# x's split straight from PSUM at two joins, the second half's turn half a unit later, and other banks for the HGRN values

## The reference, cut to what matters

```python
x = x + gate[:, None, :] * y            # after each mixer of the first block
...
x = _rms_norm(x, final_g)               # the first block's output
...
u = rmsnorm(h, norm1_w[l])
proj = jnp.einsum('bsd,de->bse', u, w_in[l])
...
h = h + jnp.einsum('bse,ed->bsd', mixed, w_out[l])
u2 = rmsnorm(h, norm2_w[l])
gu = jnp.einsum('bsd,df->bsf', u2, w_gate_up[l])
```

## Time and profile before

| | us |
|---|---|
| median of 3 runs (726.63 to 727.56) | 727.55 |
| the profiled execution | 727.51 |
| its span, first to last instruction | 725.7 |
| TensorE busy, matmuls / weight loads | 705.6 / 577.7 |
| VectorE busy | 501.6 |
| ScalarE busy | 380.0 |

### The profile page before, as it was taken

The page is one execution under the profiler, slowest core; times in us unless marked ns, Lnnn a source line. Parts: engine busy times, 40 slices in busy tenths (PEclk is TensorE's granted clock), DMA queues, the critical chain, the costliest instruction groups (busy, mean ns, idle before and its releaser), DMA issues.

```text
span 725.7 us, 9362 instructions
## 1 busy us (share of the span) xinstructions
PE 705.6 (97%) x3534; PEld 577.7 (80%) x3534; DVE 501.6 (69%) x727; ACT 380.0 (52%) x559; POOL 15.9 (2%) x33
## 2 busy tenths in 40 slices
PE   6999999999999999999999899999999999999996
PEld 5887877777887788788887688878888888888884
DVE  4789888787956778665658689955775555555444
ACT  5347544565544565553565654554565445444342
POOL 6000000000000000000000000000000000000000
PEclk8799999999999999999999999999999999999999
DMA  9998865676986357733444553333456655555611
GB/s 295 369 373 312 295 202 182 197 227 210 312 296 205 113 178 249 244 117 115 147 148 143 146 174 117 117 116 117 129 187 206 192 180 180 180 196 178 197 61 58
DMA packets 74476, 138.96 MB, mean 191 GB/s; under 512 B 5748, under 2 KB 18272, under 8 KB 74432
## 3 DMA queue, kind: packets, MB, share of 16 engines
q1 hardware_dynamic: 72816, 134.82, 57.3%
q10 hardware_dynamic: 736, 1.90, 0.7%
q0 software_dynamic: 880, 1.64, 0.6%
HBM read 137.31 MB, written 1.05 MB: 191 GB/s over the span
## 4 chain that ended last, share of the span: by engine, by line
PE 89%; DVE 6%; ACT 2%; issue 2%; DMA 1%; SPq 0%; DVEq 0%; ACTq 0%
PE G L382 23%; PE G L384 23%; PE G L383 22%; PE T L403 5%; PE T L771 2%; DVE wlo L1057 2%; PE T L884 2%; DVE arena L1057 1%; PE T L761 1%; PE G L493 1%; DMA arena<-in_mod_w_dram 1%; PE G L495 1%; PE G L494 1%; PE T L444 1%; ACT whi L1796 1%
## 5 line engine op out<-in xcount | busy, mean ns | idle before, releaser
L1057 DVE TENSOR_TENSOR wlo<-raw,whi 128x1024 fp32r<-128x1024 f32 x202 | 246.1, 1223 | 127.2 <-ACT whi L1796 126.5
L382 PE MATMUL G<-whi,ahi 128*128 128x512 f32 x760 | 307.8, 405 | 4.3 <-DVE wlo L1057 4.3
L384 PE MATMUL G<-whi,alo 128*128 128x512 f32 x760 | 297.0, 391 | 0.0
L383 PE MATMUL G<-wlo,ahi 128*128 128x512 f32 x760 | 296.1, 390 | 0.0
L1796 ACT ACTIVATE whi<-raw 128x1024 fp32r<-128x1024 f32 x202 | 212.9, 1060 | 123.5 <-PE G L384 108.4
L382 PEld LDWEIGHTS G<-whi,ahi 128*128 128x128 f32 x760 | 142.9, 188 | 36.9 <-DVE wlo L1057 8.9
L384 PEld LDWEIGHTS G<-whi,alo 128*128 128x128 f32 x760 | 142.6, 188 | 31.3
L383 PEld LDWEIGHTS G<-wlo,ahi 128*128 128x128 f32 x760 | 143.1, 188 | 28.0 <-issue 1.2
L1798 ACT ACTIVATE arena<-T,st 128x128 f32<-128x128 f32 (+2 forms) x56 | 21.7, 478 | 30.4 <-DVE st L1429 30.4
L1796 ACT ACTIVATE ahi<-T 128x512 fp32r<-128x512 f32 x25 | 15.0, 599 | 41.8 <-PE T L403 41.8
L403 PE MATMUL T<-head,arena 128*128 128x128 f32 x244 | 36.8, 275 | 0.0
(11 more groups left out here) (227 smaller groups left out, 606.8 us busy)
## 6 DMA issues: line engine op xcount, KB each, us to landing
raw<-in_ret_w_in_dram SPq DMA_DIRECT2D x48, 512.0 KB, 5.4
raw<-in_w_gate_up_dram SPq DMA_DIRECT2D x40, 512.0 KB, 3.6
raw<-in_mod_w_dram SPq DMA_DIRECT2D x32, 512.0 KB, 4.8
raw<-in_fox_w_in_dram SPq DMA_DIRECT2D x32, 512.0 KB, 4.8
raw<-in_w_in_dram SPq DMA_DIRECT2D x28, 512.0 KB, 3.5
raw<-in_w_down_dram SPq DMA_DIRECT2D x22, 512.0 KB, 4.3
arena<-in_mod_w_dram SPq DMA_DIRECT2D x16, 512.0 KB, 8.8
raw<-in_ret_w_out_dram SPq DMA_DIRECT2D x16, 512.0 KB, 5.6
```

What stands on the lines that cost most here:

```text
L382: e.matmul(o, ah, wh, start=first and k == 0, stop=False)
L383: e.matmul(o, ah, wl, start=False, stop=False)
L384: done = e.matmul(o, al, wh, start=False, stop=last and k == 1)
L1057: e.tensor_tensor(o, a, b, op).then_inc(sig[name], 1)
```

## The change

`x_high` on ScalarE and `x_low` on VectorE take the place of `x_act` and `x_split` for n = 4 to 11. `x_high` writes the scaled, rounded tiles straight to `ahi`; `x_low` computes tile * scale - `ahi` from PSUM, one `scalar_tensor_tensor` for each 128x128 tile, and waits for all four activations of its n. The stage isn't used any more. `ready` names one count per tile, and the T bank of these n is free only when `x_low` is through with it. In unit 1 of the second block the second turn of x's second half comes between the products of m = 0 and m = 1. `x_low(7)` stands behind the first `f_prod`, `x_high(7)` behind the first `square`, and ScalarE squares `f_prod` k one loop turn later. `hg_values` uses banks 1 and 2 by name, so the rotation behind it begins two banks earlier. The numbers computed are the same; no load is changed. (The own tiles for the forgetting attention's first chunk, `own_tiles`, are in both kernels.)

```diff
             def x_turn(src, k0, m):
...
-                t = bank(("x", n), sig["x_act"], 2 * SPLIT_ORDER.index(n) + 2)
+                p = SPLIT_ORDER.index(n)
+                t = bank(("x", n), *((sig["x_act"], 2 * p + 2) if n < 4 else (sig["x_split"], 4 * p + 4)))
...
-                for z in range(2):
-                    for k in range(2):
-                        ready[slot + k0 + 2 * z + k, m] = (sig["x_split"], 4 * p + 3 + z)
+                for k in range(4):
+                    ready[slot + k0 + k, m] = (sig["x_split"], 4 * p + (3 + k // 2 if n < 4 else 1 + k))
...
             for k in range(4):
-                unit(u, accs, 16 + 2 * k, k == 0, k == 3)
-                u += 1
-                if k == 0:
-                    for m in range(2):
-                        on_.wait_ge(sig["res1"], 2 * m + 6)
-                        x_turn(x, 4, m)
+                for m in range(2):
+                    products(u, m, accs, 16 + 2 * k, k == 0, k == 3)
+                    if (k, m) in ((0, 1), (1, 0)):
+                        on_.wait_ge(sig["res1"], 2 * k + 6)
+                        x_turn(x, 4, k)
+                u += 1
...
-                t = bank(("hg_values", m), sig["hg_norm"], 4 + m)
+                t = bank(("hg_values", m), sig["hg_norm"], 4 + m, 1 + m)
...
+            def x_low(n, slot, k0, m, scale):
...
+                on_.wait_ge(sig["x_act"], 2 * p + 2)
+                for k in range(4):
+                    b = slot + k0 + k
+                    stt(alo[:, b, ms], t[:, k * P:(k + 1) * P], scale(k0 + k), ahi[:, b, ms].bitcast(F32), ALU.mult, ALU.subtract, "x_split")
...
-            x_split(4, 16, 0, 0, stage2)
-            x_split(5, 16, 0, 1, stage2)
+            x_low(4, 16, 0, 0, lambda k: col(n1f, k))
+            x_low(5, 16, 0, 1, lambda k: col(n1f, k))
...
                 if k == 0:
-                    x_split(6, 16, 4, 0, stage2)
-                    x_split(7, 16, 4, 1, stage2)
+                    x_low(6, 16, 4, 0, lambda k: col(n1f, k))
...
                 tt(f2[:, m, cs_], x[:, m, cs_], fg[:, cs_], ALU.mult, "f_prod")
+                if k == 0:
+                    x_low(7, 16, 4, 1, lambda k: col(n1f, k))
...
+            def x_high(n, slot, k0, m, scale):
...
+                on_.wait_ge(sig["x_turned"], n + 1)
+                for k in range(4):
+                    act(ahi[:, slot + k0 + k, ms], t[:, k * P:(k + 1) * P], ACT.Copy, "x_act" if k % 2 else None, scale=scale(k0 + k))
...
-            x_act(6, stage2, 4, ACT.Copy, lambda k: col(n1f, k))
-            x_act(7, stage2, 4, ACT.Copy, lambda k: col(n1f, k))
+            x_high(6, 16, 4, 0, lambda k: col(n1f, k))
             on_.wait_ge(sig["left_turned"], 12)
             for k in range(4):
...
                 square(c, m, 1, 2 * k + 2)
-                on_.wait_ge(sig["f_prod"], k + 1)
-                on_.wait_ge(sig["sq1"], k + 1)
-                act(xn1[:, m, cs_], f2[:, m, cs_], ACT.Square, "sf1", accum=st[:, 68 + 2 * m + c:69 + 2 * m + c])
+                if k == 0:
+                    x_high(7, 16, 4, 1, lambda k: col(n1f, k))
+                if k:
+                    square_f(k - 1)
+            square_f(3)
```

More of the change, by code:

```diff
@@ L1186, in x_split @@
                     tt(alo[:, b:b + 2, ms], stage[:, (2 * p + z) % 4, :, :], ahi[:, b:b + 2, ms].bitcast(F32), ALU.subtract, "x_split")
+            def x_low(n, slot, k0, m, scale):
+                p = SPLIT_ORDER.index(n)
+                t, ms = T[bank_of["x", n]], slice(m * P, m * P + P)
+                on_.wait_ge(sig["x_act"], 2 * p + 2)
+                for k in range(4):
+                    b = slot + k0 + k
+                    stt(alo[:, b, ms], t[:, k * P:(k + 1) * P], scale(k0 + k), ahi[:, b, ms].bitcast(F32), ALU.mult, ALU.subtract, "x_split")
             stage1 = acc[:, 2048:3072].rearrange("p (z n s) -> p z n s", z=4, n=2)
@@ L1498, in _ @@
             u_out = {0: u + 1, 1: u + 3}
-            stage2 = gate[:, 0, :].rearrange("p (z n s) -> p z n s", z=4, n=2)
             ring_to(u + 2)
@@ L1719, in _ @@
             ring_to(u + 4)
-            x_split(8, 22, 0, 0, stage2)
-            x_split(9, 22, 0, 1, stage2)
+            x_low(8, 22, 0, 0, lambda k: col(n2_col, k))
+            x_low(9, 22, 0, 1, lambda k: col(n2_col, k))
             ring_to(u + 5)
@@ L1745, in _ @@
                     if c == 0 and k == 0:
-                        x_split(10, 22, 4, 0, stage2)
-                        x_split(11, 22, 4, 1, stage2)
+                        x_low(10, 22, 4, 0, lambda k: col(n2_col, k))
+                        x_low(11, 22, 4, 1, lambda k: col(n2_col, k))
                     if c == 0 and k == 2:
@@ L2114, in _ @@
             sqrt_table()
-            stage2 = gate[:, 0, :].rearrange("p (z n s) -> p z n s", z=4, n=2)
             ring_to(u + 4)
             on_.wait_ge(sig["rows_read"], 3)
-            x_act(4, stage2, 0, ACT.Copy, lambda k: col(n1f, k))
-            x_act(5, stage2, 0, ACT.Copy, lambda k: col(n1f, k))
+            x_high(4, 16, 0, 0, lambda k: col(n1f, k))
+            x_high(5, 16, 0, 1, lambda k: col(n1f, k))
             ring_to(u + 5)
@@ L2143, in turned_win, with square_f @@
                 from_four("wqk", n, (qA, kA)[n // 2][:, :, m * P:(m + 1) * P], ACT.Copy, (0.125, 1.0)[n // 2])
+            def square_f(k):
+                c, m = k // 2, k % 2
+                cs_ = slice(512 * c, 512 * c + 512)
+                on_.wait_ge(sig["f_prod"], k + 1)
+                on_.wait_ge(sig["sq1"], k + 1)
+                act(xn1[:, m, cs_], f2[:, m, cs_], ACT.Square, "sf1", accum=st[:, 68 + 2 * m + c:69 + 2 * m + c])
             ring_to(u + 2)
             u += 1
-            x_act(6, stage2, 4, ACT.Copy, lambda k: col(n1f, k))
-            x_act(7, stage2, 4, ACT.Copy, lambda k: col(n1f, k))
+            x_high(6, 16, 4, 0, lambda k: col(n1f, k))
             on_.wait_ge(sig["left_turned"], 12)
@@ L2243, in _ @@
             ring_to(u + 4)
-            x_act(8, stage2, 0, ACT.Copy, lambda k: col(n2_col, k))
-            x_act(9, stage2, 0, ACT.Copy, lambda k: col(n2_col, k))
+            x_high(8, 22, 0, 0, lambda k: col(n2_col, k))
+            x_high(9, 22, 0, 1, lambda k: col(n2_col, k))
             ring_to(u + 5)
@@ L2257, in _ @@
                     if c == 0 and k == 0:
-                        x_act(10, stage2, 4, ACT.Copy, lambda k: col(n2_col, k))
-                        x_act(11, stage2, 4, ACT.Copy, lambda k: col(n2_col, k))
+                        x_high(10, 22, 4, 0, lambda k: col(n2_col, k))
+                        x_high(11, 22, 4, 1, lambda k: col(n2_col, k))
                         on_.wait_ge(sig["left_turned"], 16)
```

## The result

The changed kernel took 721.96 us (median of 4 runs, 721.78 to 723.09) against 727.55 us (4 runs, 726.63 to 729.19): ratio 0.9916 [0.9898, 0.9935]. That is 5.6 us faster by the medians and 6.1 us by the ratio. The forecast was 721.8. Repeated on another chip it was 722.11 us (5 runs) against 727.81 (9 runs), ratio 0.9921 [0.9905, 0.9936].

What follows compares the result with a forecast made beforehand. TensorE, busy 97% of the span, was taken as the bound, so time is gained only where it waits. Join 4.9 plus HGRN banks 0.8 plus feed-forward 0 gave 5.7 us: 727.5 to 721.8 us, range 720.7 to 723.7.

Steps and rivals of the forecast that it cites:

- What bounded the kernel: Join from forgetting attention to second block: TensorE waits 5.6 of 30.3 us, mostly on a 3.64 us round trip.
- The split: VectorE's x_low from PSUM: four operations at 0.27 us pitch, 1.08 us per n; alone costs 0.16 us before first turn.
- Rival A: At x_low: short operations don't overlap, pitch 0.35 us, gain only 4.6 us, giving 722.9 us; chance 0.15.
- The turn half a unit later: Second turn of x's second half, at the join: its 0.91 us wait disappears at no cost.
- ScalarE's order: Second block's loop at the join: a ScalarE round takes some 2.2 us, under TensorE's 2.72.
- One of the prediction's signs of being wrong: At the join: rounds of over 2.8 us between whi starts would show the forecast wrong.
- The q turns: Turns of q at the join's end: put_h and q products, 5.0 us earlier, stop holding them; up to 0.35 us more.
- The banks: HGRN values in banks 1 and 2: their wait behind the last window-attention product goes, gaining 0.8 us.
- Rival C: At the HGRN values: the bank does nothing because another wait stands behind it, 722.6 us; chance 0.09.
- The feed-forward join: Same split at n = 8 to 11: additions 0.16 us later, unseen by TensorE; 0, at most 0.3 us lost.
- Rival B: Mixers, VectorE full from 434 to 444 us: they take the gain back, only 0.8 us stays, 726.7 us; chance 0.08.
- Rival D: The 16 x_low operations before a wlo at the join: pitch above 0.63 us erases the gain; 729.5 us at 0.75; chance 0.03.

Runs made afterwards that it cites:

- e8: Changed kernel with e7's edit, f_prod and its squares one more loop turn later, put_h(1) and feed-forward squares also later: 720.55 us, repeated 720.76 us.
- e4: Kernel before the change, with only the squares of f_prod moved one loop turn later on ScalarE: 723.61 us, ratio 0.9933.
- e3: Changed kernel with each f_prod squared in its own loop turn again: 727.09 us, ratio 0.9976.
- e6: Changed kernel with each of the 16 x_low operations of n = 4 to 7 issued twice on VectorE: 725.73 us (one run).
- e2: Changed kernel with both turns of x's second half behind unit 0 again: 722.24 us, ratio 0.9912.
- e7: Changed kernel with VectorE's first addition of x's second half put before the wlo it stood behind: 721.66 us (one run).
- e1: Changed kernel with the HGRN values' banks taken from the rotation again: 723.38 us, ratio 0.9930.
- e5: Changed kernel with the old order of squares, n = 7, turns and banks, leaving only the split from PSUM: 727.81 us, ratio 0.9993.

## Why the prediction was right

**What bounded the kernel.** Right. Of the 5.6 us counted as waiting 5.2 went, and e8, in which no weight load of the join waits, has a stretch 5.65 us shorter than before's: the count was right. The round trip was the cause of most of it: taking it out alone removed M3 to M7's five waits (e4), putting it back alone brought them back (e3).

**The split.** The pitch was forecast at 0.27 us and a duration of 347 ns. VectorE after, two timeline rows and the group's row with its mean, then ScalarE:

```profile
388.58 2.16 DVE L1066 SCALAR_TENSOR_TENSOR alo<-T,n1f,ahi 128x128 fp32r<-128x128 f32 x8 [0.81 <-ACT ahi L1805]
390.65 1.21 DVE L1057 TENSOR_TENSOR wlo<-raw,whi 128x1024 fp32r<-128x1024 f32 x1
...
L1066 DVE SCALAR_TENSOR_TENSOR alo<-T,n1f,ahi 128x128 fp32r<-128x128 f32 x16 | 4.4, 342 | 0.8 <-ACT ahi L1805 0.8
```

```profile
387.40 2.17 ACT L1805 ACTIVATE ahi<-T,n1f 128x128 fp32r<-128x128 f32 x8 [2.04 <-PE T L403]
```

Eight in 2.16 us with a last one of 0.34 are seven pitches of 0.26: they overlap by 0.08, as the earlier trace rows had it for 256 columns. Rival A is out. By the rule weighed in the prediction (the Trainium skill, VectorE: DVE Perf Modes, section The DRAIN you can't avoid) they would start 0.34 apart. The same section says further that a next operation that is not held starts earlier, which the prediction left out. The rows fit that: each of these operations starts 0.08 before the end of the one in front, here and in e6. The activations, costed at nothing, took 2.17 for 2.18.

The step's own number, 0.16 us later in front of the first turn, was too dear. The split of n = 5 ends 3.34 us after ScalarE's start, against 3.21 before: 0.13 later. But `wlo` begins 0.09 before it ends (390.65 against 388.58 + 2.16), where before it began 0.02 behind the subtraction's end. So the additions came as early as before, and the first turn waited 0.38, not 0.54.

**The turn half a unit later.** Right: no second wait. M2 starts 10.18 us behind the first half's turn, forecast 10.38, the 0.16 of the first wait among it.

**ScalarE's order.** A round of 2.18 us, forecast 2.2, is under TensorE's 2.72:

```profile
396.77 1.07 ACT L1805 ACTIVATE whi<-raw 128x1024 fp32r<-128x1024 f32 x1
...
398.95 1.06 ACT L1805 ACTIVATE whi<-raw 128x1024 fp32r<-128x1024 f32 x1
...
401.12 1.06 ACT L1805 ACTIVATE whi<-raw 128x1024 fp32r<-128x1024 f32 x1
```

One of the prediction's signs of being wrong, a round of over 2.8 us between `whi` starts in M3 to M6, did occur. M6's copy starts 3.66 us behind M5's (the last row above), because ScalarE waits for the last `f_prod`:

```profile
404.15 0.63 ACT L1803 ACTIVATE acc<-arena 128x512 f32<-128x512 f32 x1 [0.74 <-DVE arena L1057]
...
404.78 1.05 ACT L1805 ACTIVATE whi<-raw 128x1024 fp32r<-128x1024 f32 x1
```

This is the last round trip, which the prediction's own working left standing: there M5's copy starts at 399.6 and M6's near 403.2, so the sign contradicted the working. TensorE doesn't see it: M6's `wlo` ends at 407.16, and M6 starts at 407.63 without a wait.

M3 was to wait 0.19 for `wlo`; it is held by 0.06. VectorE was early by the same 0.16, and by an overlap between the split of n = 7 and that `wlo` (398.24, 0.09 before the split's end). M7 started 5.10 us earlier (23.82 us behind the first half's turn, 28.92 before), forecast 4.75. The difference is the first wait's 0.16 and M3's 0.13, and some hundredths.

**The q turns.** This step failed. "VectorE is then 5.0 earlier, so `put_h` and the q products, which come 5.0 earlier too, no longer hold the q turns" compares VectorE with where it was, and not with TensorE, which had come forward by as much. VectorE's second q product was 5.2 earlier (it starts the row at 416.11), M7 5.1: a wait between two engines that move together stays. The row:

```profile
416.11 1.40 DVE L1061 TENSOR_SCALAR arena<-G,st 128x512 f32<-128x512 f32 x2
```

The waits are 0.24 and 0.24, against 0.38 and 0.24. They go only in runs in which TensorE comes later against VectorE (e2, e4, e6), or VectorE's q products come earlier against TensorE (e7, e8). That the join's sum stood all the same is luck: the q turns gave 0.10 where up to 0.35 was hoped for, and M7 was 0.35 earlier than forecast; 5.20 measured for 4.9.

**The banks.** 0.86 for 0.8, nothing behind it. Rival C is out (e1).

**The feed-forward join.** 0, as forecast: the second half's turn doesn't wait, and the two waits for `wlo` that were there stay (0.29 and 0.41, before 0.30 and 0.43).

**Rival B**, the mixers take it back: M9 to L771 is 82.06 us for 82.12, and between them no weight load has a wait of over 0.2 us that it hadn't before. **Rival D**: 0.24 to 0.26 us an operation (e6), where 0.63 was the point from which it decides.

The parts sum to 6.1 us, the medians to 5.6, the forecast to 5.7. The half microsecond between traces and medians is inside the ratio's interval (4.7 to 7.4 us of 727.55, the ratio itself being 6.1), and nothing here tells whether it is given back anywhere: the rest of the trace is 6.1 shorter in both traces of the changed kernel. So the mechanism was right but for the q turns, and that the median came within 0.2 us of the forecast is in part luck, since the parts gave 0.4 us more than forecast.

## What to carry to other kernels

Where engines exchange work in a loop and each runs its own order, add up the round trip (product, square, copy, subtraction) before the busy times: at 3.64 us it held a loop of 2.72 although neither engine was full, and moving the consumer one turn back, three lines, was four fifths of the join's gain. When a stage moves, ask of each wait behind it whether both sides move; then it stays. And where single parts are worth half a microsecond of 720, measure them as lengths between two instructions of the trace, since the opening varies by more.

## What the runs showed of the hardware that I had not expected

**A wait in front of short transposes costs less than its bracket.** Four transposes with no wait keep the weight loads for 0.55 us (394.90 to 395.45), four behind a wait for 0.39 (393.24 to 393.63). In e7 the turn starts at 6.36 us behind the first half's turn and the next load at 6.91; in the changed kernel, with its 0.38 of waiting, at 6.70 and 7.09. So the bracket of 0.38 cost 0.18 in all. The two q waits of 0.24 likewise: that unit with its turns takes 3.89 us with them (M8 to M9, after) and 3.63 without (e8), 0.26 for 0.48. This is why e8's stretch ended at 30.96 where I had taken the brackets off in full.

**The opening varies.** All kernels here run the same instructions up to the first half's turn, and their profiled executions reach it between 383.78 us (e5) and 387.11 (e1), 3.3 us apart, more than any part of the change but one. The whole spread is there at the eight transposes near 236 us already (234.55 in e5, 237.90 in e1). The granted clock of the first 60 us was 0.86, 0.89, 1.00 and 1.00 in four of them (after, before, e8 and e1), which reach the turn at 386.54, 384.82, 384.86 and 387.11; so the clock alone doesn't order them, and what does stays open.
